# Half of each expert's down product as three products of high and low parts

## What is computed

```
xs = hpad[slot_tok].reshape(n_blocks, DISPATCH_BLOCK, D)      # blocks of 128 tokens
def expert_block(args):
    xb, e = args
    return (jax.nn.silu(xb @ w_gate[e]) * (xb @ w_up[e])) @ w_down[e]
yb = lax.map(expert_block, (xs, block_expert)).reshape(cap, D)
out = jnp.zeros((T + 1, D), jnp.float32).at[slot_tok].add(yb.astype(jnp.float32) * slot_w[:, None])
```

## Time and profile before

| | |
|---|---|
| time, median of 3 runs | 1425.97 us (1424.84 to 1427.04) |
| profiled execution, its own time | 1427.76 us |
| span of the profile | 1426.0 us |
| PE busy | 1287.0 us, 90% |
| DVE busy | 969.6 us, 68% |
| ACT busy | 618.0 us, 43% |
| POOL busy | 160.6 us, 11% |
| mean granted TensorE clock | 0.950 |
| DMA | 347.81 MB, mean 244 GB/s |

### The profile page before, as it was taken

One profiled execution on the slowest core, in us unless ns is written; L12 is line 12 of the kernel. 1 busy time (PEld: TensorE's weight loads), 2 busy tenths in 40 slices (PEclk: granted clock), 3 DMA queues, 4 the chain that ended last, 5 costly groups with the idle time before them and its releaser, 6 DMA issues.

```text
span 1426.0 us, 14722 instructions
## 1 busy us (share of the span) xinstructions
PE 1287.0 (90%) x5057; PEld 864.6 (61%) x5057; DVE 969.6 (68%) x1379; ACT 618.0 (43%) x795; POOL 160.6 (11%) x169
## 2 busy tenths in 40 slices
PE   2999899949999999987999999998499999999886
PEld 2566665536666667743788854467367666667432
DVE  8678875576777777726766587856667777776153
ACT  3486401235555555504222167734355555554002
POOL 6000000010000000011000057710100000000200
PEclk9999899969999999999899999999599999999999
DMA  9636674258999999894365230024589999998641
GB/s 352 227 111 244 221 278 164 94 200 300 370 365 366 368 377 376 308 362 150 103 252 177 89 118 1 1 74 159 220 317 372 376 369 364 372 376 304 232 188 59
DMA packets 78114, 347.81 MB, mean 244 GB/s; under 512 B 12500, under 2 KB 12684, under 8 KB 69104
## 3 DMA queue, kind: packets, MB, share of 16 engines
q1 hardware_dynamic: 67184, 325.70, 61.4%
q0 software_dynamic: 7344, 16.68, 3.3%
q10 hardware_dynamic: 3536, 4.79, 0.9%
HBM read 334.15 MB, written 23.07 MB: 251 GB/s over the span
## 4 chain that ended last, share of the span: by engine, by line
PE 77%; DVE 12%; ACT 4%; DMA 4%; issue 2%; POOL 0%; SPq 0%; DVEq 0%; ACTq 0%; POOLq 0%
PE ps L1911 24%; PE ps L1922 16%; PE ps L2023 9%; PE ps L1831 4%; PE ps L1902 3%; PE ps L1793 3%; PE ps L1838 2%; PE ps L1897 2%; PE ps L1798 2%; DVE scratch L1027 2%; PE ps L2067 2%; PE ps L2095 2%; PE ps L2081 2%; DMA x_res<-in_x_dram 1%; DVE slab_ring_r L1449 1%
## 5 line engine op out<-in xcount | busy, mean ns | idle before, releaser
L1922 PE MATMUL ps<-slab_ring,scratch 128*128 128x512 f32 x560 | 246.5, 593 | 3.4 <-ACT scratch L935 2.1
L1911 PE MATMUL ps<-slab_ring_r,gate_rows_r 128*128 128x512 f32 x512 | 202.1, 395 | 0.0
L1922 PEld LDWEIGHTS ps<-slab_ring,scratch 128*128 128x128 f32 x560 | 105.8, 190 | 124.2 <-issue 117.2
L1449 DVE TENSOR_TENSOR slab_ring_r<-slab_ring,h_t_r 128x2048 fp32r<-128x2048 f32 x64 | 143.9, 2288 | 16.8 <-ACT h_t_r L852 16.8
L2023 PE MATMUL ps<-slab_ring_r 128*128 128x512 f32 x384 | 123.1, 402 | 4.1 <-DVE h_t_r L1084 4.1
L852 ACT ACTIVATE h_t_r<-slab_ring 128x2048 fp32r<-128x2048 f32 x64 | 118.6, 1901 | 0.0
L1911 PE MATMUL ps<-h_t_r,gate_rows_r 128*128 128x512 f32 x256 | 105.7, 413 | 12.5 <-issue 7.6
L881 ACT ACTIVATE scratch<-ps,mod_ab 128x128 f32<-128x128 f32 x128 | 48.1, 456 | 143.8 <-PE ps L1897 143.8
L1911 PEld LDWEIGHTS ps<-slab_ring_r,gate_rows_r 128*128 128x128 f32 x512 | 97.9, 191 | 19.2 <-issue 0.5
L1911 PE MATMUL ps<-h_t_r,scratch_r 128*128 128x512 f32 x256 | 102.9, 402 | 0.0
L1449 DVE TENSOR_TENSOR slab_ring_r<-slab_ring,mod_ring_r 128x2048 fp32r<-128x2048 f32 x32 | 73.3, 2292 | 41.0 <-ACT mod_ring_r L852 41.0
(11 more groups left out here) (343 smaller groups left out, 2303.0 us busy)
## 6 DMA issues: line engine op xcount, KB each, us to landing
slab_ring<-in_expert_w_gate_dram SPq DMA_DIRECT2D x35, 2048.0 KB, 9.5
slab_ring<-in_expert_w_up_dram SPq DMA_DIRECT2D x35, 2048.0 KB, 9.9
slab_ring<-in_expert_w_down_dram SPq DMA_DIRECT2D x35, 2048.0 KB, 9.7
mod_ring<-in_mod_w_dram SPq DMA_DIRECT2D x40, 512.0 KB, 4.5
y_rows<-scratch SPq DMA_DIRECT2D x32, 512.0 KB, 10.3
slab_ring<-in_mod_w_dram SPq DMA_DIRECT2D x32, 512.0 KB, 4.8
slab_ring<-in_mod_w_dram SPq DMA_DIRECT2D x12, 1024.0 KB, 11.5
slab_ring<-in_w_qkv_dram SPq DMA_DIRECT2D x6, 2048.0 KB, 12.0
```

The lines of the kernel that those rows point to most:

```text
L1449: tt_(rest, w, top.bitcast(F32), ALU.subtract).then_inc(low_ready[c], 1)
L1911: ins = pe.matmul(ps[:, bank, :], x, w, start=(kt == 0 and i == 0), stop=(kt == KT - 1 and i == 2))
L1922: ins = pe.matmul(ps[:, 5 + h, :], hidT[:, f, :], w[:, 2 * f + h, :], start=(f == 0), stop=(f == FT - 1))
```

## The change

The contraction of the down product has four parts f of 128. Parts 2 and 3 stay plain float32 matmuls. Parts 0 and 1 become split products: three float32r matmuls for each of the two parts and the two output halves, 12 in place of 4 plain ones. TensorE does the four plain ones first and waits for the low parts (`down_rest`, `hid_rest`) between the two kinds.

New on ACT: `high_down`, a copy of 128 x 2048 weights, after `high(0, e + 1)` and ahead of `xst(e + 1)`; and `take_hid` makes two copies of 128 x 256 (one into `hid_high`) in place of one of 128 x 512. New on DVE: `low_down(e - 1)`, a subtraction of 128 x 2048 and one of 128 x 256 out of PSUM, between the two chunks of `low(1, e)`. The high parts lie in `modr_r` in layer 0 and in the buffer of the normalized tokens in layer 1, half of it for each parity. The transfers and their conditions stay as they are. Three semaphores of the setup are merged into others, since three new ones are needed.

```diff
+    down_high = [(modr_r, XN_r[:, :, :].rearrange("p t (h n) -> p (t h) n", h=2))[l] for l in range(LAYERS)]
+    hid_high = R_r[:, 8, 0:2 * P].rearrange("p (f n) -> p f n", n=P)
+    hid_low = R_r[:, 15, 2 * P:4 * P].rearrange("p (f n) -> p f n", n=P)
...
+    def down_split_of(l, par):
+
+        return slab(("exp", l, 2, par))[:, 0:FT, :], down_high[l][:, FT * par:FT * par + FT, :], w_low(l, 2, par)[:, 0:FT, :]
...
-                act.activation(hidT, ps[:, 4, :].rearrange("p (f n) -> p f n", n=P), ACT.Copy).then_inc(hidt_ready, 1)
+                act.activation(hid_high, ps[:, 4, 0:2 * P].rearrange("p (f n) -> p f n", n=P), ACT.Copy)
+                act.activation(hidT[:, 2:FT, :], ps[:, 4, 2 * P:4 * P].rearrange("p (f n) -> p f n", n=P), ACT.Copy).then_inc(hidt_ready, 1)
+
+            def high_down(e, par, turn, first=0):
+
+                wait_slab(act, ("exp", l, 2, par), turn)
+                if first == 1:
+                    act.wait_ge(xn_stored, 16 * TT * (l + 1))
+                if not first:
+                    act.wait_ge(down_done, e + (e0 - 1))
+                w, top, _ = down_split_of(l, par)
+                act.activation(top, w, ACT.Copy).then_inc(down_top, 1)
...
                 if not last:
                     for chunk in range(2):
                         high(0, e + 1, 1 - par, turn + par, chunk)
-                    if first != 1:
-                        xst(e + 1, 1 - par)
+                high_down(e, par, turn, first)
+                if not last and first != 1:
+                    xst(e + 1, 1 - par)
...
+            def low_down(e, par):
+
+                v.wait_ge(down_top, e + (e0 + 1))
+                w, top, rest = down_split_of(l, par)
+                tt_(rest, w, top.bitcast(F32), ALU.subtract).then_inc(down_rest, 1)
+                v.wait_ge(hidt_ready, e + (e0 + 1))
+                tt_(hid_low, ps[:, 4, 0:2 * P].rearrange("p (f n) -> p f n", n=P), hid_high.bitcast(F32), ALU.subtract).then_inc(hid_rest, 1)
+
             def step(e, par, stored=None, first=False, last=False):
-                for chunk in range(2):
-                    low(1, e, par, chunk)
+                low(1, e, par, 0)
+                if not first:
+                    low_down(e - 1, 1 - par)
+                low(1, e, par, 1)
...
             step(NE - 1, 1, NE // 2 - 1, last=True)
+            low_down(NE - 1, 1)
             take_y(NE - 1, 1, NE // 2 - 1)
...
                 wait_slab(pe, ("exp", l, 2, par), turn)
-                down(slab(("exp", l, 2, par)), down_done)
+                w, w_top, w_rest = slab(("exp", l, 2, par)), down_high[l][:, FT * par:FT * par + FT, :], w_low(l, 2, par)
+                for h in range(2):
+                    for f in range(2, FT):
+                        pe.matmul(ps[:, 5 + h, :], hidT[:, f, :], w[:, 2 * f + h, :], start=(f == 2), stop=False)
+                pe.wait_ge(down_rest, e + (e0 + 1))
+                pe.wait_ge(hid_rest, e + (e0 + 1))
+                for h in range(2):
+                    for f in range(2):
+                        top, rest = w_top[:, 2 * f + h, :], w_rest[:, 2 * f + h, :]
+                        for i, (x, y) in enumerate(((hid_high, top), (hid_high, rest), (hid_low, top))):
+                            ins = pe.matmul(ps[:, 5 + h, :], x[:, f, :], y, start=False, stop=(f == 1 and i == 2))
+                ins.then_inc(down_done, 1)
```

More of the change, by code:

```diff
@@ L236, in build @@
     mask_base = sem("mask_base")
-    mask_ready = sem("mask_ready")
-    cs_ready = sem("cs_ready")
     cols_turned = sem("cols_turned")
     table_args, table_values = sem("table_args"), sem("table_values")
-    dec_ready = sem("dec_ready")
     x_ready = sem("x_ready")
@@ L263, in build @@
     down_done, yb_ready = sem("down_done"), sem("yb_ready")
+    down_top, down_rest, hid_rest = sem("down_top"), sem("down_rest"), sem("hid_rest")
     yb_stored = [sem("yb_stored0"), sem("yb_stored1")]
@@ L652, in _ @@
             link(gp.tensor_tensor(LC[:, :], LC[:, :], part, ALU.add))
-        gp.sem_inc(mask_ready, 1)
+        gp.sem_inc(consts_ready, 1)
         def gathers(l):
@@ L732, in _ @@
             act.wait_ge(c_loaded, 16)
-            act.activation(cs[:, :], cT[:, :], ACT.Silu).then_inc(cs_ready, 1)
+            act.activation(cs[:, :], cT[:, :], ACT.Silu).then_inc(table_values, 1)
             load(mbc[:, :, :], a["mod_b"].rearrange("l (q p k) -> p (l q) k", p=P, k=KT))
@@ L811, in _ @@
         high_in(2, 1)
-        act.wait_ge(mask_ready, 1)
-        act.wait_ge(dec_ready, 1)
+        act.wait_ge(consts_ready, 3)
+        act.wait_ge(table_args, 3)
         def take_z(t):
@@ L1108, in _ @@
         v.sem_inc(mask_base, 1)
-        v.wait_ge(cs_ready, 1)
+        v.wait_ge(table_values, 1)
         mod_acc(0, 0, 8)
@@ L1157, in _ @@
         v.sem_inc(table_args, 1)
-        v.wait_ge(table_values, 3)
+        v.wait_ge(table_values, 4)
         e_, s_, t_, y_ = lru[:, 1, :], lru[:, 2, :], lru[:, 3, :], lru[:, 4, :]
@@ L1172, in _ @@
         link(ts(dec[:, 2, :], t_, -8.0, None, ALU.mult))
-        ts(dec[:, 1, :], t_, 4.0, None, ALU.mult).then_inc(dec_ready, 1)
+        ts(dec[:, 1, :], t_, 4.0, None, ALU.mult).then_inc(table_args, 1)
         def col(i):
@@ L1704, in low_wo @@
             tt_(rest, plain, top.bitcast(F32), ALU.subtract).then_inc(o_low, 1)
-        v.wait_ge(mask_ready, 1)
+        v.wait_ge(consts_ready, 3)
         for i in range(LAST + 1):
```

## The result

| | before | after |
|---|---|---|
| median of four runs each, us | 1425.9 | 1405.93 |
| lowest to highest | 1424.84 to 1427.04 | 1405.48 to 1406.42 |
| span of the profiled execution (its own time) | 1426.0 (1427.76) | 1403.7 (1405.48) |
| distance of two down products, mean of 28 | 19.15 | 18.46 |

The two medians are 20.0 us apart. The ratio of the runs is 0.9854 with an interval of [0.9842, 0.9866], which is 20.8 us less, between 19.1 and 22.5. The forecast was 20.9. The changed kernel was run once more, beside the last experiments: 1404.45 us against 1427.0, 0.9844 [0.9831, 0.9858]. Each ratio further on is against runs of the kernel before made beside it, whose median was 1426.91, 1427.2 or 1427.0 us.

A forecast was written before the change was run, and what follows sets the result against it. TensorE was taken to bound the kernel without pause in the inner steps. 0.67 us times 30 steps plus 0.8 at the layers' ends, 20.9 us, took 1425.97 to 1405.1 us; range 1402.5 to 1411.

The forecast's parts named there:

- The bound: Inner steps of both layers: TensorE's work alone sets the 19.14 us step, so time off TensorE shortens the end.
- TensorE's product: Down product in each step: 6.17 us in place of 6.87, 0.70 us less.
- The passage: Switch from plain to float32r matmuls inside the down product: costs 0.01 to 0.05 us, taken as 0.03.
- The layer ends: Last down product of each layer: 0.70 us gained less 0.32 for ACT's split copy, 0.38 us, twice, 0.8 us.
- The sum: Whole kernel: 0.67 us times 30 steps, 20.1, plus 0.8 at the layers' ends, 20.9 us saved.
- DVE fits: DVE's chain in each step: new subtractions fill gaps, everything after stands 0.44 us later, 0.35 us of slack left.
- The rival of DVE's bound: DVE's chain 0.76 us longer than counted: step 18.88 us, gain 8.6, 1417 us; half way 1411; chance 0.11.
- The added waits: TensorE's wait for low parts has 2.5 us to spare, ACT's new copy 1.1, the down slab at least 4.4.
- The transfers: Loads within a layer: 381 GB/s needed against a full rate of 379, lag 1.3 us over 13 steps, no cost.
- the rival: Transfers bind at a full rate of 368 GB/s: lag 8.7 us per layer less 4.4 slack, 1413.7 us; chance 0.05.
- Slower: ACT's new copy waits for a down slab landing over 20 us after issue; at 22 us, 1478 us; chance 0.03.
- no change: DVE's chain in each step is longer by 0.7 plus 0.35 us, leaving 1426 us; chance 0.03.

The follow-up runs named there:

- the two halves of the change run apart: Changed kernel without its new ACT and DVE work: 1349.46 us, not comparable, steps 18.44 to 18.48; with that work but eight plain matmuls: 1428.23 us.
- both experiments that lengthen DVE's chain: Changed kernel with one more 128 x 256 subtraction on DVE per step: 1407.63 us; with two of 128 x 512 besides: 1424.32 us.
- With the cover gone: Changed kernel with DVE's two new subtractions after both chunks of up's low parts: 1452.63 us, ratio 1.0181.
- more bytes: Changed kernel with each output block stored twice, 0.52 MB more per step: 1405.58 us, ratio 0.9849.
- more work on DVE: Changed kernel with three more subtractions on DVE per step, its chain 1.67 us longer: 1424.32 us, ratio 0.9981.

## Why the prediction was right, point by point

- **The bound.** Right. TensorE is without a pause in the inner steps, and the two halves of the change run apart show that it is TensorE's part alone that gives the gain.
- **TensorE's product.** Forecast 6.17 us, measured 3.43 + 2.74 = 6.17. The passage was put at 0.03 and is not more than 0.01: the steps are 0.69 shorter, not 0.67. That is 0.6 us over 30 steps, to the good.
- **The layer ends.** In proportion, the term that was mis-sized most. The delay by ACT's split copy was taken as 0.32 us, from starts 0.42 apart and 0.50 for the second copy; they are 0.28 apart and 0.38 long, so the second ends 0.66 after the first began where one copy took 0.60, and the product starts 0.07 later. A copy of half the width lets the next start after 0.28 us, where the full width took 0.50. Each end gained about 0.6 us (0.70 - 0.07, seen in the distance of the last two products: 14.51 to 13.87), not 0.38.
- **The sum.** 28 distances x 0.69 + 2 x 0.64 for the last distance of each layer + 2 x 0.68 for the last products = 22.0 us, against 22.3 between the two spans, 20.8 by the ratio, whose interval reaches from 19.1 to 22.5, and 20.0 between the medians. The forecast of 20.9 was some 1 us below what the steps and ends add up to, less than these runs can tell. That it stands within 0.1 us of the ratio's 20.8 is luck; what the runs bear out is its terms.
- **DVE fits.** Right, but its slack has another composition. The small subtraction is 0.42 us as interpolated. The chain ended sooner than laid out, 15.63 us after its start in place of 15.86, since the cast takes 0.43 us where the step of before on which I built had 0.68 (from 499.72 on, beside GpSimd's indirect DMA from 499.15 on, rows below). Against that, I set the slack against the matmul; the weight load 0.22 us earlier is what waits, and the signal takes 0.18 us, not 0.04. Left are 0.2 us instead of 0.35.

```profile
499.72 0.68 DVE L1480 CAST gate_rows_r<-scratch 128x512 fp32r<-128x512 f32 x1
499.15 1.02 POOL L671 DMA_INDIRECT scratch<-xn_rows,gather_idx  x1 [0.85 <-POOL gather_idx L669]
```

- **The rival of DVE's bound.** Its mechanism was shown, by both experiments that lengthen DVE's chain, but its price was wrong by a factor of two. "Each further tenth takes 3 us" holds a step for closed; TensorE's wait gives DVE a head start, so a tenth costs 1.5. The 1417 us of that rival would have been about 1411.
- **The added waits.** Right: TensorE never waits for the low parts, ACT has 1.05 us to spare (forecast 1.1), and the slab is there long before. The low parts are there at 484.97 and 485.30, and TensorE asks at 487.79: the 2.5 us of cover that were forecast. With the cover gone the kernel is slower than before.
- **The transfers.** No loss, as forecast, but the reasoning behind the rival was wrong: dividing 368 GB/s by a busy share of 0.97 gives no full rate, which was to be 379. The share is 0.99 at 383 and 1.01 at 404 GB/s. The Trainium skill, "DMA: Bandwidth & Descriptors", section "Where 436 GB/s comes from", would have had HBM bind at about 358 GB/s; the windows with 383, 398 and 404 GB/s don't agree for one core working alone. The Trainium skill's same page has, in the section "Measured", 425 GB/s for 16 MB on a single core, and about 358 for each only when both cores of a pair stream. The 415 in the last quarter with more bytes is in accord with that; no run here reaches 425 in a stretch of that length or has a second core at work.
- **Slower, and no change.** Neither condition was near. The down slabs landed after 10.2 us in the median of the window, against the 16.4 us at which ACT asks for one and the 20 us from which the slower case would have begun.

## What to carry to other kernels

Where one engine is busy without a pause, price a change by what it takes off that engine, and then lay the neighbours' chains end to end in order of time: 28 us more of DVE's sum in twelve steps (194.29 against 166.71) cost nothing, while two subtractions moved one place down its order cost 47 us over the kernel. Where a neighbour's chain was longer than the step by d, it cost d / 2 in the mean if it started from an event ahead of the wait that it caused, and the whole wait in every step if it started behind it. A busy share near 1 of the transfers did not tell what they could still carry (368 GB/s at 0.97, 404 at 1.01); add bytes and look at the rate and at the landings.

## What the runs showed of the hardware that I had not expected

- **GpSimd and DVE lock each other out.** A cast of 0.43 us took 4.81 beside a GpSimd subtraction of 4.57. The other way round, with more work on DVE, GpSimd's small copy (0.18 to 0.27 us in the changed kernel, up to 1.90 here) was held up by DVE's pair of subtractions, which ran from 359.73 to 364.22:

```profile
362.36 1.90 POOL L674 COPY gather_idx<-slot_token 128x1 int32 x1 [16.20 <-PE ps L1929]
```

  It ended at 364.26. The Trainium skill, "SBUF — State Buffer", section "SBUF: two separate sides", describes a pair of ports that the two engines share and that one holds for a whole instruction; the ends of both rows agree with that.
- **A wait of TensorE costs more than the idle time that the profile gives.** With idle times of 0.80 to 1.41 us, at a clock of 1.00, the step lost 0.24 to 0.28 us more. The starts show two sources of it in the step read above: the idle time is counted from the end of a record that would have overlapped the next, 0.16 us, and the first matmul, whose weight load was not done ahead of it, is 0.11 us further from the second. With 3.20 us idle it lost 1.86 more, with the clock below 1.00.
- **The transfers of one core** went up to 404 GB/s in the mean of twelve steps, at landings of the down loads that rose from 12.0 to 15.4 us (medians of the first and the last quarter).
